# Two edits to a two-block transformer kernel: the order of transfers and buffers in its modulation stage, and four tiles' residual and norms placed in the second half of the feed-forward

## The reference, cut to what matters

```
mod   = silu(c) @ w_mod + b_mod          # six rows of 1024; mod_c the same from c_ctx
sh1, sc1, g1, sh2, sc2, g2 = split(mod)
h     = x * (1 + sc1) + sh1              # also for the context, with mod_c
y     = concat(mlstm(h), sgu(h), conv(h), s5(h)) @ w_out
x     = layer_norm(ALPHA * x + g1 * y, ln1_w, ln1_b)
x     = layer_norm(ALPHA * x + g2 * swiglu(x * (1 + sc2) + sh2, w_ffn_in, w_ffn_out), ln2_w, ln2_b)
```

## Time and profile before

| | |
|---|---|
| median of 3 runs | 2402.72 us (2401.91 to 2403.92) |
| the profiled execution's own time | 2400.59 us |
| its span | 2398.8 us |
| TensorE busy in the span | 2161.2 us |
| VectorE, ScalarE, POOL busy | 1250.8, 697.3, 396.5 us |
| modulation stage | 0 to 60.5 us |
| feed-forward, second half, hidden part | about 1092 to 1330 us |
| end of the first block | 1452.3 to 1522 us |

### The profile page before, as it was taken

The page is one execution under the profiler, slowest core; times in us unless marked ns, Lnnn a source line. Parts: engine busy times, 40 slices in busy tenths (PEclk is TensorE's granted clock), DMA queues, the critical chain, the costliest instruction groups (busy, mean ns, idle before and its releaser), DMA issues. The chain is left out here.

```text
span 2398.8 us, 27818 instructions
## 1 busy us (share of the span) xinstructions
PE 2161.2 (90%) x10421; PEld 1594.0 (66%) x10421; DVE 1250.8 (52%) x2238; ACT 697.3 (29%) x1240; POOL 396.5 (17%) x469
## 2 busy tenths in 40 slices
PE   4998989986988999999999994658999887999998
PEld 2854464475447888888888884635888774657876
DVE  4672794257673333223333227369999563763433
ACT  2222111021002222222232223263212243761325
POOL 0920011032000000000000002300692551300110
PEclk9999999998998999999999997777999998998999
DMA  6543110002214333334333333100111102003201
GB/s 255 185 124 106 48 58 1 0 1 97 71 53 123 96 96 92 90 110 137 96 96 93 89 90 105 54 14 23 48 48 48 44 1 78 1 2 123 70 1 70
DMA packets 185194, 176.17 MB, mean 73 GB/s; under 512 B 12726, under 2 KB 157430, under 8 KB 181770
## 3 DMA queue, kind: packets, MB, share of 16 engines
q1 hardware_dynamic: 179114, 165.99, 22.3%
q0 software_dynamic: 2304, 8.39, 0.9%
q10 hardware_dynamic: 3680, 0.54, 0.1%
HBM read 160.98 MB, written 12.60 MB: 72 GB/s over the span
## 5 line engine op out<-in xcount | busy, mean ns | idle before, releaser
L1653 DVE TENSOR_TENSOR ff_part<-ff_raw,ff_part 128x1024 fp32r<-128x1024 f32 (+2 forms) x152 | 165.0, 1085 | 458.4 <-ACT ff_part L1604 458.4
L1527 PE MATMUL ps<-h,ff_part 128*128 128x512 f32 x704 | 274.8, 390 | 4.0 <-DVE ff_part L1653 4.0
L1604 ACT ACTIVATE ff_part<-ff_raw 128x1024 fp32r<-128x1024 f32 (+2 forms) x152 | 144.4, 950 | 449.1 <-PE ps L1529 447.2
L1528 PE MATMUL ps<-h,ff_part 128*128 128x512 f32 x704 | 274.4, 390 | 0.0
L1529 PE MATMUL ps<-h,ff_part 128*128 128x512 f32 x704 | 274.3, 390 | 0.0
L1527 PE MATMUL ps<-pj_part,h 128*128 128x512 f32 (+1 forms) x448 | 174.8, 390 | 12.7 <-POOL pj_part L2042 8.4
L1528 PE MATMUL ps<-pj_part,h 128*128 128x512 f32 (+1 forms) x448 | 174.2, 389 | 0.0
L1529 PE MATMUL ps<-pj_part,h 128*128 128x512 f32 (+1 forms) x448 | 174.2, 389 | 0.0
L2101 DVE TENSOR_SCALAR_CACHE_REDUCE pj_junk<-NM,prm 128x384 uint8<-128x384 f32 (+1 forms) x186 | 163.7, 943 | 1.1
L1527 PEld LDWEIGHTS ps<-h,ff_part 128*128 128x128 f32 x704 | 132.5, 188 | 32.0 <-DVE ff_part L1653 4.5
L1529 PEld LDWEIGHTS ps<-h,ff_part 128*128 128x128 f32 x704 | 132.5, 188 | 27.6
(11 more groups left out here) (548 smaller groups left out, 3981.6 us busy)
## 6 DMA issues: line engine op xcount, KB each, us to landing
ff_raw<-in_w_ffn_in SPq DMA_DIRECT2D x88, 512.0 KB, 3.7
s_wm<-in_w_mod SPq DMA_DIRECT2D x16, 1024.0 KB, 4.8
ff_raw<-in_w_ffn_out SPq DMA_DIRECT2D x32, 384.0 KB, 3.3
pj_raw<-in_w_in SPq DMA_DIRECT2D x48, 256.0 KB, 2.6
ff_raw<-in_w_ffn_out SPq DMA_DIRECT2D x32, 320.0 KB, 3.1
mod_w<-in_w_mod SPq DMA_DIRECT2D x8, 1024.0 KB, 8.2
mod_x<-in_x SPq DMA_DIRECT2D x8, 512.0 KB, 8.8
w_out<-in_w_out SPq DMA_DIRECT2D x4, 1024.0 KB, 8.7
```

Source lines behind the costliest of these rows:

```text
L1527: nc.tensor.matmul(out, w[0], x[0], start=first, stop=False)
L1528: nc.tensor.matmul(out, w[0], x[1], start=False, stop=False)
L1604: nc.scalar.activation(part[s % 2][0][:, 0:n, :], raw[s][:, 0:n, :], ACT.Copy).then_inc(hi, 1)
L1653: v.tensor_tensor(part[s % 2][1][:, 0:n, :], raw[s][:, 0:n, :], part[s % 2][0][:, 0:n, :].bitcast(F32), ALU.subtract).then_inc(lo, 1)
```

## The change

In the modulation stage: ScalarE's queue issues the three small parameter transfers (A and the time step) first, ahead of its Silu, on `S["in"]`, and the other eight on a semaphore of their own, `S["cin"]`. VectorE's chain waits for the three. TensorE transposes A before the first weight slice, C behind the last one; VectorE's copies of C stand at the end of its chain. The bias matmuls stand behind the fourth slice. Two of the four pairs of row sums go through VectorE instead of ScalarE. The ten tiles have ten buffers, SP issues them without a wait, and the next stage's weight behind them.

In the feed-forward: the hidden part of the second half is written out instead of looped, for ScalarE, VectorE and TensorE. In its rounds stand, for tiles 0 to 3 (the first half of the tokens, which is ready): the transposes back (rounds 0, 2, 4, 6, into banks 6 and 7), the residual and statistics, the affine part, the square and roots, and the weighing with `norm_mix`, which writes over the tile in `ynT`. POOL's queue stores the rows to `x2` and fetches the rows of x1 for tiles 2 to 5. The end stage does the whole only for tiles 4 to 7 and transposes the first four from `ynT`. The clearing of the semaphores stands ahead of the feed-forward instead of behind the end stage.

```diff
@@ stage_modulate, SP
             for i in range(tiles):
-                if i >= NX:
-                    sp.wait_ge(h_tr, (i - NX) // 2 + 1)
-                if i == NX:
-                    sp.wait_ge(w_use, KT)
-                    sp.dma_start(Z.wd[:], ...).then_inc(K.s5_in, 16)
-                sp.dma_start(xr[i % NX][:], src(i)).then_inc(x_in[i % NX], 16)
+                sp.dma_start(xr[i][:], src(i)).then_inc(x_in[i // 2], 16)
+            sp.wait_ge(w_use, KT)
+            sp.dma_start(Z.wd[:], ...).then_inc(K.s5_in, 16)
@@ stage_modulate, ScalarE
-            act.wait_ge(c_in, 16 * 2)
-            nc.scalar.activation(K.cols[:], K.cols[:], ACT.Silu).then_inc(c_act, 1)
             for a, name in enumerate(("s5_a_re", "s5_a_im")):
                 act.dma_start(Z.araw[:, a, :], ...).then_inc(S["in"], 16)
             act.dma_start(Z.ldt[0:N2, :], ...).then_inc(S["in"], 16)
+            act.wait_ge(c_in, 16 * 2)
+            nc.scalar.activation(K.cols[:], K.cols[:], ACT.Silu).then_inc(c_act, 1)
...
@@ stage_modulate, VectorE
             s5_parameters(K, dve, Link(nc.vector, S["chain"]), S)
+            dve.wait_ge(w_use, KT)
+            dve.wait_ge(consts, 4)
+            for j in range(2, 4):
+                r = slice(32 * j, 32 * j + 2)
+                nc.vector.tensor_copy(sums[r, :], K.bank[7][r, :]).then_inc(row_ev, 1)
@@ s5_parameters
-    dve.wait_ge(S["in"], 16 * 11)
+    dve.wait_ge(S["in"], 16 * 3)
...
+    dve.wait_ge(S["part"], 2)
+    for h in range(2):
+        link(v.tensor_copy(Z.Cm[h * SN:(h + 1) * SN]..., K.bank[5][h * SN:(h + 1) * SN, :]...))
@@ stage_ffn, VectorE
+            def norm(i):
+                x = K.fe_x[i % 2]
+                dve.wait_ge(E["back"], i + 1)
+                dve.wait_ge(K.fe_x_in[i] if i < 2 else K.fe_y_in[i % 2], 16)
+                for b in range(2):
+                    c = slice(b * HALF, (b + 1) * HALF)
+                    last = v.scalar_tensor_tensor(out=x[:, c], in0=x[:, c], scalar=ALPHA, in1=K.bank[6 + b][:], op0=ALU.mult, op1=ALU.add)
+                last.then_inc(E["x"], 1)
...
+                        if h and j == 0 and r in (3, 5, 7, 9):
+                            weigh((r - 3) // 2)
+                        elif h and j == 1 and r < 8:
+                            norm(r // 2) if r % 2 == 0 else spread(r // 2)
@@ stage_ffn, ScalarE
+                        if h and j == 0:
+                            if r % 2 and r < 8:
+                                act.wait_ge(E["sq"], r)
+                                nc.scalar.activation(rs, rs, ACT.Sqrt).then_inc(E["sq"], 1)
+                            elif r in (2, 4, 6, 8):
+                                i = r // 2 - 1
+                                act.wait_ge(E["x2"], i + 1)
+                                rms_root(K, act, wide(K.fe_x[i % 2][:]), rows_of(i), ss[:, i:i + 1], E["ss"], i)
@@ stage_ffn, TensorE
+                        if h and j == 0 and r in (0, 2, 4, 6):
+                            back(r // 2)
...
-                loop(pe, hidden, NF // FT)
+                loop(pe, hidden, NF // FT, unrolled=(h == 1))
@@ stage_ffn, POOL
+            for i in range(4):
+                pool.wait_ge(E["x2"], i + 1)
+                pool.dma_start(K.x2[i * P:(i + 1) * P, :], K.fe_x[i % 2][:]).then_inc(stored[i % 2], 16)
+                pool.wait_ge(stored[i % 2], 16 * (i // 2 + 1))
+                pool.wait_ge(E["h"], i + 1)
+                pool.dma_start(K.fe_x[i % 2][:], K.x1[(i + 2) * P:(i + 3) * P, :]).then_inc(K.fe_y_in[i % 2], 16)
@@ stage_first_end, VectorE
-            for i in range(NT):
-                norm(i)
-                if i:
-                    inverse(i - 1)
-                if i >= 3:
-                    low(i - 3)
...
+            norm(0)
+            low(0)
+            low(1)
+            inverse(0)
+            norm(1)
+            low(2)
+            low(3)
+            inverse(1)
+            norm(2)
+            low(4)
...
@@ build
-        if stage is stage_first_end:
+        if stage is stage_join:
             nc.clear_and_free_semaphores(K.sems)
```

More of the change, by code:

```diff
@@ L220, in stage_modulate @@
     w_use, mc_tr, row_ev, mc_ev = (K.sem("mod_" + n) for n in ("use", "mtr", "rev", "mev"))
-    x_in = [K.sem(f"modx_in{s}") for s in range(NX)]
+    x_in = [K.sem(f"modx_in{g}") for g in range(NG)]
     h_tr, h_act, h_dve = K.sem("h_tr"), K.sem("h_act"), K.sem("h_dve")
-    S = K.s5S = {n: K.sem("s5p_" + n) for n in "in ldtx part sinin sinout rot chain bychain pchain".split()}
+    S = K.s5S = {n: K.sem("s5p_" + n) for n in "in cin ldtx part sinin sinout rot chain bychain pchain".split()}
     K.s5_in = K.sem("s5_in")
@@ L311, in _ @@
             pe.wait_ge(consts, 3)
+            pe.wait_ge(S["ldtx"], 1)
+            for a in range(3):
+                last = nc.tensor.transpose(K.bank[4][:, a * N2:(a + 1) * N2], Z.araw[:, a, :], K.ident[0:N2, 0:N2])
+            last.then_inc(S["part"], 1)
             pe.wait_ge(c_act, 1)
@@ L357, in mod_rows @@
         mm = K.nc.tensor.matmul(bank[32 * j:32 * j + 2, :], K.cols[:, :, t], w[:, j * HALF:(j + 1) * HALF],
-                                start=first, stop=(not first and t == KT - 1 and bank is not K.bank[7]))
+                                start=first, stop=(t == KT - 1))
     return mm
@@ L1550, in stage_ffn @@
     g2_tr = K.sem("ff_g2")
+    K.x2 = nc.dram_tensor("x2", (T, D), F32, kind="Internal").ap()
     K.fe_x = [K.at(f"fe_x{s}", kb, [P, D]) for s, kb in enumerate((144, 20, 88))]
+    E = {n: K.sem("ff_e" + n) for n in "back x sq x2 ss h chain".split()}
+    stored, K.fe_y_in = [K.sem(f"ff_st{s}") for s in range(2)], [K.sem(f"ff_yin{s}") for s in range(2)]
+    st, mv, rs, ss = K.prm[:, 0:12].rearrange("p (a b) -> p a b", a=2), K.prm[:, 12:14], K.prm[:, 14:15], K.prm[:, 16:20]
     K.fe_rows = K.at("fe_rows", 132, [P, 3, D])
@@ L1557, in stage_ffn, with first, loop, rows_of @@
     w2 = I["w_ffn_out"][0].rearrange("(f p) n -> p f n", p=P)
-    def loop(eng, body, count):
+    def first(r):
+        return isinstance(r, int) and r == 0
+    def loop(eng, body, count, unrolled=False):
         body(0)
-        with eng.Fori(1, count) as r:
-            body(r)
+        if unrolled:
+            for r in range(1, count):
+                body(r)
+        else:
+            with eng.Fori(1, count) as r:
+                body(r)
+    def rows_of(i):
+        return K.ynT[:, 0, :, i * P:(i + 1) * P]
+    def wide(x):
+        return x.rearrange("p (k n) -> p k n", k=KT)
     def unit(h, r, c):
@@ L1677, in output @@
                             split(u + s, s, QUART[s + 1] - QUART[s])
-                            if s == 1 and m == 0 and isinstance(r, int):
+                            if s == 1 and m == 0 and first(r):
                                 multiply(h, u - 1, NF - 1, 1)
-                loop(dve, hidden, NF // FT)
+                loop(dve, hidden, NF // FT, unrolled=(h == 1))
                 loop(dve, output, KT // 2)
@@ L1688, in _, with back @@
             last.then_inc(g2_tr, 1)
+            def back(i):
+                pe.wait_ge(oev, KT)
+                if i:
+                    pe.wait_ge(E["x"], i)
+                for k in range(KT):
+                    last = nc.tensor.transpose(K.bank[6 + k // 4][:, (k % 4) * P:(k % 4 + 1) * P], K.ynT[:, 0, k, i * P:(i + 1) * P], K.ident[:])
+                last.then_inc(E["back"], 1)
             for h in range(2):
@@ L1838, in low @@
                                     ALU.subtract).then_inc(tev, 1)
-            dve.wait_ge(r_in, 48)
-            for i in range(NT):
-                norm(i)
-                if i:
-                    inverse(i - 1)
-                if i >= 3:
-                    low(i - 3)
-            inverse(NT - 1)
-            low(NT - 3)
-            low(NT - 2)
-            low(NT - 1)
+            norm(0)
[8 more added lines that the diff above has]
+            low(4)
+            inverse(2)
+            norm(3)
+            low(5)
+            inverse(3)
+            low(6)
+            low(7)
 PJ_KB, FREE_KB, SMALL_KB = 88, 24, 18
```

224 lines of the change are left out of this document (130 added, 94 removed).

## The result

The changed kernel takes 2378.55 us (median of 4 runs, 2377.86 to 2380.34) against 2402.34 of before, run beside it (4 runs, 2401.91 to 2403.92): ratio 0.990, 95% interval 0.9886 to 0.9914. That is 23.8 us less where 38.5 were forecast: 14.4 us above the predicted 2364.2 and 1.5 above the range. The profiled execution took 2380.34, 1.8 over its median where that of before was 2.1 under its own, so the two traces show 20.2 us of difference in span.

The account below looks back on a forecast made before the run. TensorE, busy nine tenths of the span, bounds the kernel; time is won where it idles. -14.5 + 3.9 - 27.9 = -38.5 us, from median 2402.72 to 2364.2; range 2356 to 2377.

Parts of the forecast that it names:

- Part 1: Modulation stage: earlier parameter chain and weights at DMA speed start the next stage at 46.0 instead of 60.5, gain 14.5 us.
- The sine: Modulation stage, a cover: ScalarE issues until 21.5, VectorE needs 7.2 more, so 28.7 against C's 29.5.
- the sign of this failure: Modulation stage, listed as showing the forecast wrong: a VectorE wait for the sine's root that ends after 30 us.
- C "there" at 29.5: Modulation stage: last weight's rows done at 28.4, four transposes of C take 1.1, so C is ready at 29.5 us.
- the longer bound: Modulation stage: last weight at 28, first group's transposes at the lower clock throughout, 3.9; next stage at 48.6, gain 11.9.
- the forecast 46.0: End of the modulation stage: the next stage starts at 46.0 us instead of 60.5.
- The modulation stage stays bound by something else: Rival: sine behind ScalarE's queue, or transposes at lower clock; modulation gains 7 instead of 14.5 us, total 2372; chance 0.15.
- that cover: Modulation stage: the sine ready at 28.7 before C at 29.5; if lost, the sum moves by the excess only.
- Part 2: Feed-forward: four tiles' transposes cost TensorE 3.9 us; the rest is free, insertions of up to 5.1 us fitting.
- Part 3: First block's end: only four tiles done whole, stage ends at 1494.1 instead of 1521.98, gain 27.9 us.
- the clearing: Clearing semaphores moves from behind the first block's end to ahead of the feed-forward: 1.5 us leave and come, sum zero.

Follow-up runs that it names:

- e2: The changed kernel with the modulation stage of the kernel before, so the feed-forward part alone: 2379.02 us, ratio 0.9893 to the kernel before.
- e9: The kernel before with only the hidden-layer loop of the feed-forward's second half written out: 2404.99 us, ratio 1.0006 to the kernel before.
- e1: The kernel before with the modulation edit alone: 2403.51 us, ratio 0.9999 to the kernel before.
- e3: The changed kernel with B, D and bias on their own semaphore, so C waits only for its own transfers: 2376.40 us, ratio 0.9885 to before.
- e8: e4 with POOL's issues behind the last weight's rows and VectorE's row sums ahead of its copies of C: 2363.16 us, ratio 0.9832 to before.
- e4: e3 with B, D and the bias column issued on POOL's queue instead of ScalarE's: 2367.45 us, ratio 0.9849 to the kernel before.
- e7: e3 with B alone on POOL's queue, D and bias on ScalarE's ahead of the sine: 2365.99 us, ratio 0.9843 to before.
- e5: The changed kernel with SP asking for the token tiles only after all eight later parameter transfers landed: 2366.56 us, ratio 0.9842 to before.
- e6: e3 with B, D and bias issued behind the sine on ScalarE's queue: 2369.78 us, ratio 0.9852 to the kernel before.

## Why the prediction was off

**The step that failed** is in Part 1: "The sine: ScalarE's queue issues transfers until 21.5, then VectorE needs the part from 36.05 to 43.21, that is 7.2, so 28.7, against 29.5 when C is there." The 7.2 held (33.85 to 41.00 is 7.15). The 21.5 was a reading of the kernel before, where B's issue ends at 18.1 and D's takes 2.9; in the changed kernel the three issues end at 33.31. These are the rows of before, ScalarE's issues and the DMA engines' pause behind them:

```profile
6.70 0.60 ACTq L273 DMA_DIRECT2D s_B<-in_s_b_re  x1
7.33 10.77 ACTq L273 DMA_DIRECT2D s_B<-in_s_b_im  x1
...
18.12 2.92 ACTq L274 DMA_DIRECT2D s_D<-in_s_d  x1
```

```profile
20.00:28.80 8.80, 4.72 (x27) 1.75 (x31) 2.95 (x14) 0.00 (x0) 0.00 (x0) 1.00 0.22 37
```

I took the lengths as properties of the transfers and moved them into a kernel in which the DMA engines have no such pause (407 GB/s from 20 to 30 us, where before has 37; the prediction itself says that they starve there). The same prediction counted the fuller traffic as its gain and kept the queue behind it at the price of the emptier one. The trace had a row against it, which I didn't read for this: the first transfer of B is issued in 0.60 us and the second, of the same size and shape, in 10.77. That is no cost of issuing, it is a wait, and a wait moves with what it waits for. The prediction had also named the sign of this failure, a VectorE wait for the root of the sine that ends after 30; it ended at 33.85.

The excess of that step, and of one beside it, account for the stage. VectorE's copies of C start at 43.43 instead of 29.5: 11.5 us from the sine (chain's end 41.0 instead of the 29.5 that C set) and 2.4 from the count of eight. The prediction had C "there" at 29.5 without asking what its wait counts: the same queue's last transfer. The last 1.2 us are sizes: the row sums with their gaps 0.5 over, and from the start of the sums' transposes to the first eviction 4.6 (45.99 to 50.62) where I had 3.9, since the first group's transposes run at a granted clock of 0.50 throughout, as the longer bound had it. 11.5 + 2.4 + 1.2 = 15.1, and the next stage starts 15.1 us after the forecast 46.0.

That this nearly equals the 14.4 us of the medians is in part luck. The two traces miss the forecast by 18.3 us of span, and 3.8 of it lie in stages that the prediction left alone. The S5 stage takes 181.9 us (61.0 to 242.9) where it took 179.6; its first 19.0 us, at granted clock 1.00, became 20.6 at 0.92, and so they did in e2, but not in e9. The mixers behind it take 333.1 us (242.9 to 576.0) where they took 331.6, in every kernel with the modulation edit (e1, e3 to e8: 333.1 to 333.3) and in none without it (e2 and e9: 331.6 and 331.7); TensorE is busy there 1.7 us longer for the same matmuls, at a mean granted clock of 0.95 instead of 0.96 in the later 240 us. What makes the difference no run shows.

**The rival** "The modulation stage stays bound by something else" was the right one and was named with this very queue "beside more traffic". Its size was wrong: it kept 7 of the 14.5 us, and e1 shows that nothing was left. With all 14.5 gone the sum gives 2378.7, and 2378.55 was measured. "If that cover goes, the sum moves by the excess only" was right, and the excess was the whole gain.

**What held.** The rest of Part 1: e4 and e7 take the issue out of the way and reach 46.7 for 46.0. Part 2: 3.5 us for the transposes against 3.9, no wait of TensorE behind twelve insertions, and the loop's form worth nothing (e9). Part 3: 28.9 against 27.9, and the clearing sums to zero. Together 24.0 forecast, and 24.0 measured by e2; the match to the decimal is luck, since its two parts in the traces give 28.9 - 3.5 = 25.4 and e2's interval is 21 to 30.

The table load takes 1.28 us and the root follows 0.01 us behind it, so the drain that "ScalarE: Activation LUTs" of the Trainium skill, section "What ACT_TABLE_LOAD costs", adds shows in no row of the change either. The Trainium skill's page "DMA: Bandwidth & Descriptors", section "Issuing engines are not separate DMA queues", says that spreading issues over engines saves only the sequencer's time to initiate a transfer, usually small beside the transfer. These traces don't agree for B and what stands behind it: the initiation took 27 us of ScalarE's time, three issues together, and moving it was worth 11.9 us of the stage (58.6 to 46.7).

## What to carry to other kernels

Read the length of every issue instruction as you read a wait. One that is long for its bytes may be a wait for other transfers, as B's was here, and it holds everything behind it on that engine, computation included. When a change fills a pause of the DMA engines, ask which issue ended in that pause. Put a transfer of many small pieces on the queue of an engine that has nothing to compute, or behind the operation that others wait for. And a wait on a count of many transfers is a wait for the last of them, however early the wanted ones land.

## What was unexpected in the hardware

The same two transfers of B show this, from the profile's rows on their landing (least, median and largest us from issue to landing), for the kernel before, the changed one, and e4:

```profile
DMA to landing us min/median/max: 14.0/14.4/14.7
```

```profile
DMA to landing us min/median/max: 30.0/32.2/34.3
```

```profile
DMA to landing us min/median/max: 7.2/7.3/7.4
```

From ScalarE's queue they landed after 14 us with a pause in the traffic and after 30 to 34 without one; from POOL's queue, beside the full weight stream, after 7. The issue of the second blocked ScalarE 10.77 us, 16.65 us, and POOL 0.90. The profile counts 12726 packets under 512 bytes in the whole changed kernel and 10439 in e4, so the two queues also cut the transfers differently. What exactly fills up, a queue's room for pieces or something shared with the weights' queue, no run here tells. Full DMA engines alone don't explain the length: they moved 424 GB/s from 16 to 18 us in the kernel before, and B's issue ended there at 18.1; in the changed kernel they moved 410, and it went on to 22.9. What differs is how much was still queued, six weight slices before, and in the change all eight and, from 16.7 us on, the tiles. e5 and e6 fit a block that ends when earlier work has drained, but they don't show it directly.

TensorE's clock in this stage is not fixed by the code. e2 has the modulation code of before, and its next stage starts at 63.6 us instead of 60.5. The two stretches, of before and of e2:

```profile
43.00:60.00 17.00, 10.74 (x83) 9.88 (x81) 9.39 (x22) 9.62 (x22) 0.00 (x0) 0.93 0.51 187
```

```profile
43.00:62.00 19.00, 14.28 (x83) 13.62 (x81) 8.54 (x21) 8.56 (x20) 0.00 (x0) 0.72 0.46 170
```

The same 83 matmuls took TensorE 10.74 us at a mean granted clock of 0.93 and 14.28 at 0.72. So a difference of 2 or 3 us in this stage between two single profiles is no finding. What is said of e3 to e8 rests on when the sine, C's copies and the issues start and end; the medians of e4 to e8 lie 8.8 us or more below the changed kernel's 2378.55, while e3's 2376.40 is within the spread of both and those of e4, e5 and e7 can't be told from one another.
